# Two transformer blocks on one core: three gated tiles earlier, two memory-key tiles later, a spare expert half-slot free from the start

## What is computed

```
# first block
conv_out = conformer_conv(u_conv, ...)
attn_out = diff_attention(q, k, v, lam, ...)      # o = rms_norm(o, subln_g) per head
merged = gates[0] * (conv_out @ w_conv_out) + gates[1] * (attn_out @ w_attn_out)
x = x + merged @ w_out
h = rms_norm(x, ffn_norm_g)
x = x + hierarchical_moe(h, ...)                  # 32 experts: silu(x w_g[e]) * (x w_u[e]) @ w_d[e]
# second block
h = x
h = h + concat(mixers(rms_norm(h) @ w_in)) @ w_out
k, v = split(rms_norm(mem) @ w_kv, 2)             # memory keys and values, both 256 x 1024
h = h + softmax(q k^T) v @ w_o
h = h + conv_ffn(rms_norm(h))
return rms_norm(h)
```

## Time and profile before

| what | us |
|---|---|
| median of three runs | 1063.77 (1061.4 to 1064.07) |
| the profiled execution, by its own clock | 1061.16 |
| its span, first to last instruction | 1059.4 |
| PE busy in the span | 923.3 (87%) |
| DVE, ACT busy | 479.9 (45%), 356.7 (34%) |
| mean granted clock of TensorE | 0.939 |
| HBM read in the span | 298.9 MB |

### The profile page before, as it was taken

The page is one execution under the profiler, slowest core; times in us unless marked ns, Lnnn a source line. Parts: engine busy times, 40 slices in busy tenths (PEclk is TensorE's granted clock), DMA queues, the critical chain, the costliest instruction groups (busy, mean ns, idle before and its releaser), DMA issues.

```text
span 1059.4 us, 14271 instructions
## 1 busy us (share of the span) xinstructions
PE 923.3 (87%) x6038; PEld 669.1 (63%) x6038; DVE 479.9 (45%) x782; ACT 356.7 (34%) x569; POOL 1.3 (0%) x5
## 2 busy tenths in 40 slices
PE   7999998999889875867666776899999999999998
PEld 6969777964236431312222131389999989999986
DVE  6799867531001010010101010188866676888842
ACT  5442465131000010100000010258765745665632
POOL 0000000000000000000000000000000000000000
PEclk9999998999989997978887796999999999999999
DMA  9786230799999999999999999972334244565451
GB/s 319 272 297 244 101 119 13 296 395 421 426 411 425 419 427 424 426 427 424 427 423 429 424 428 423 406 273 81 111 128 160 80 160 160 161 207 189 160 198 40
DMA packets 76908, 300.80 MB, mean 284 GB/s; under 512 B 3761, under 2 KB 30514, under 8 KB 60210
## 3 DMA queue, kind: packets, MB, share of 16 engines
q1 hardware_dynamic: 75536, 298.89, 71.7%
q10 hardware_dynamic: 1314, 1.07, 0.4%
HBM read 298.90 MB, written 1.05 MB: 283 GB/s over the span
## 4 chain that ended last, share of the span: by engine, by line
PE 60%; DMA 27%; DVE 8%; ACT 2%; issue 1%; SPq 1%; DVEq 0%; PEldq 0%; ACTq 0%
PE bank L1361 11%; DMA ring<-in_w_down_e_dram 8%; DMA ring<-in_w_gate_e_dram 8%; DMA ring<-in_w_up_e_dram 8%; PE bank L1023 7%; PE bank L1379 6%; PE bank L1150 3%; PE bank L1243 3%; PE bank L1258 3%; PE bank L755 3%; PE bank L691 3%; PE bank L664 3%; PE bank L1076 3%; DMA qvpr<-in_w_down_e_dram 3%; DVE qvpr L1817 2%; DVE big L1916 2%
## 5 line engine op out<-in xcount | busy, mean ns | idle before, releaser
L1023 PE MATMUL bank<-ring,big 128*32 128x512 f32 x768 | 167.9, 717 | 80.9 <-DMA ring<-in_w_up_e_dram 43.0
L1023 PEld LDWEIGHTS bank<-ring,big 128*32 128x32 f32 x768 | 38.9, 127 | 202.4 <-issue 92.7
L346 DVE TENSOR_TENSOR ring_parts<-ring,ring_parts 128x2048 fp32r<-128x2048 f32 (+1 forms) x54 | 118.8, 2248 | 37.8 <-ACT ring_parts L338 37.5
L338 ACT ACTIVATE ring_parts<-ring 128x2048 fp32r<-128x2048 f32 (+1 forms) x54 | 98.5, 1874 | 53.9 <-DMA ring<-in_w_up_dram 26.0
L1361 PE MATMUL bank<-mrg_parts,ring_parts 128*128 128x256 f32 x640 | 82.3, 281 | 0.0
L2167 DVE TENSOR_TENSOR xT<-bank,xT 128x512 f32<-128x512 f32 x32 | 22.1, 692 | 130.6 <-PE bank L1062 130.6
L1361 PEld LDWEIGHTS bank<-mrg_parts,ring_parts 128*128 128x128 f32 x640 | 78.5, 189 | 0.0
L2121 DVE TENSOR_TENSOR big<-big,const 128x128 f32<-128x128 f32 x16 | 4.0, 289 | 154.4 <-PE bank L1010 154.3
L1023 PE MATMUL bank<-hs,big 128*32 128x512 f32 x128 | 70.9, 708 | 0.0
L1023 PE MATMUL bank<-qvpr,big 128*32 128x512 f32 x112 | 63.8, 725 | 1.1 <-DMA qvpr<-in_w_gate_e_dram 1.1
L2163 DVE TENSOR_TENSOR big<-bank,big 128x512 f32<-128x512 f32 x8 | 5.5, 692 | 120.2 <-PE bank L1023 120.2
(11 more groups left out here) (411 smaller groups left out, 1662.1 us busy)
## 6 DMA issues: line engine op xcount, KB each, us to landing
ring<-in_w_up_e_dram SPq DMA_DIRECT2D x24, 2048.0 KB, 29.0
ring<-in_w_gate_e_dram SPq DMA_DIRECT2D x24, 2048.0 KB, 22.0
ring<-in_w_down_e_dram SPq DMA_DIRECT2D x20, 2048.0 KB, 23.6
ring<-in_w_in_dram SPq DMA_DIRECT2D x12, 2048.0 KB, 15.0
ring<-in_w_up_dram SPq DMA_DIRECT2D x22, 1024.0 KB, 7.1
qvpr<-in_w_down_e_dram SPq DMA_DIRECT2D x5, 2048.0 KB, 20.4
ring<-in_w_down_dram SPq DMA_DIRECT2D x5, 2048.0 KB, 8.0
ring<-in_w_out_dram SPq DMA_DIRECT2D x4, 2048.0 KB, 8.4
```

Of the source, the lines that this page charges most:

```text
L338: signal(act.activation(pairs[stage][u % 3][0][:, part], raws[stage][u % 3][:, part], ACT.Copy), stage + "_hi")
L346: signal(eng.tensor_tensor(lo[:, part], raws[stage][u % 3][:, part], hi[:, part].bitcast(F32), ALU.subtract), name)
L1023: mm = pe.matmul(bank[part][CAP * j:CAP * j + CAP, :], xeT[:, c, CAP * j:CAP * j + CAP], w[j][c], start=(c == 0), stop=(c == DC - 1))
```

## The change

There are three edits.

1. `gated_conv(range(5, 8))` moves into the loop over the two head norms, behind the first.
2. Key tiles 4 and 5 leave the router's time and the tables' place. A half unit (1 MiB) is loaded at the end of turn 0 into the slot behind `KEY_UNIT`, and PE makes both tiles behind tiles 0 to 3. `RING_SHIFT` becomes 3, so that turn 1 starts one slot later. Where PE made tile 4 it now does 12 matmuls whose results nobody reads, and 4 of them where it made tile 5.
3. The tables' place is for the spare half unit alone: `load_spare(1)` stands first in `first_turn`, with no wait of its own. DVE waits for the counting matmuls before it frees `QVP`.

```diff
-            sp.dma_start(keys_w, w_xkv[:, :, 512:768]).then_inc(S["keys_early"], 16)
...
+                load_spare(1)
                 load_unit(0, 4)
...
                 load_unit(0, 7)
-                sp.wait_ge(S["keys_read"], 1)
-                load_spare(1)
                 load_unit(0, 8)
...
+                s, turn = LAST_KEYS
+                sp.wait_ge(used[s], turn + 1)
+                sp.dma_start(expert_slots[s][:, 0:2048].rearrange("p (k n) -> p k n", k=8), w_xkv[:, :, 512:768]).then_inc(landed[s], 16)
...
-        RING_SHIFT = 2
+        RING_SHIFT = 3
...
-            mem_keys((4,))
+            b = begin(pe, ("idle", 0))
+            for _ in range(12):
+                mm = pe.matmul(b[:, 0:T], ident, const[:, 0:T], start=True, stop=True)
+                tell(mm)
             pe.wait_ge(S["member"], 1)
...
-            mem_keys((5,))
+            for _ in range(4):
+                mm = pe.matmul(b[:, 0:T], ident, const[:, 0:T], start=True, stop=True)
...
                 pe.wait_ge(S["keys_full"], 4)
                 pe.sem_inc(used[s], 1)
-                pe.wait_ge(S["keys_out"], 4)
+                pe.wait_ge(S["keys_out"], 3)
+                s, turn = LAST_KEYS
+                pe.wait_ge(landed[s], 16 * (turn + (2 if s < PRELOADED else 1)))
+                w = expert_slots[s][:, 0:2048].rearrange("p (k n) -> p k n", k=8)
+                for i in range(2):
+                    for k in range(8):
+                        mm = pe.matmul(bank[0][:, T * i:T * i + T], w[:, k, P * i:P * i + P],
+                                       qko[:, k * T:k * T + T], start=(k == 0), stop=(k == 7))
+                mm.then_inc(S["keys_full"], 1)
+                pe.wait_ge(S["keys_full"], 5)
+                pe.sem_inc(used[s], 1)
+                pe.wait_ge(S["keys_out"], 5)
...
                 signal(dve.scalar_tensor_tensor(out=x, in0=x, scalar=st[:, 105:106], in1=r,
                                                 op0=ALU.mult, op1=ALU.mult), "attn_out")
-            gated_conv(range(5, 8))
+                if i == 0:
+                    gated_conv(range(5, 8))
...
+            arrive(dve, ("cnt", 0))
             dve.sem_inc(used[QVP], 1)
```

More of the change, by code:

```diff
@@ L107, in psum_plan @@
     uses += some("co", 4, 5) + some("on", 0, 2) + some("co", 5, 8) + some("mT", 0, 4) + some("ao", 0, 8) + [("rb", 0)] + some("wo", 0, 4) + some("rt", 0, 2) + some("wo", 4, 8)
-    uses += [("n2", 0)] + [None] * 3 + some("h2t", 0, 4) + some("kx", 4, 5)
-    uses += some("pos", 0, 2) + [("cnt", 0)] + some("kx", 5, 6)
+    uses += [("n2", 0)] + [None] * 3 + some("h2t", 0, 4) + [("idle", 0)]
+    uses += some("pos", 0, 2) + [("cnt", 0)]
     uses += [None] * (-len(uses) % 8)
@@ L936, in _ @@
                 scores(use, [(0, NE, C(a), mem[t], i == 0, i == len(terms) - 1) for i, (a, t) in enumerate(terms)])
-            mem_keys((5,))
+            for _ in range(4):
+                mm = pe.matmul(b[:, 0:T], ident, const[:, 0:T], start=True, stop=True)
+            filled(mm, ("idle", 0))
+            pe.sem_inc(empty[PLACE[("idle", 0)][0]], 1)
             GATHER_BANKS = (5, 6)
-            late = [("kx", 5), ("cnt", 0)]
+            late = [("cnt", 0)]
             assert not any(PLACE[use][0] in GATHER_BANKS for use in late)
-            for use in [("h2t", i) for i in range(4)] + [("mT", i) for i in range(4)] + [("rt", 0), ("rt", 1), ("n2", 0), ("kx", 4), ("pos", 0), ("pos", 1)]:
+            for use in [("h2t", i) for i in range(4)] + [("mT", i) for i in range(4)] + [("rt", 0), ("rt", 1), ("n2", 0), ("pos", 0), ("pos", 1)]:
                 copied(pe, use)
@@ L957, in _ @@
             pe.wait_ge(S["pick_step"], 2)
-            assert len(freed) == 1
+            assert not freed
             gather()
@@ L1556, in _ @@
             signal(act.activation(e_gap, e_gap, ACT.Exp), "e_exp")
-            for m in range(4, 6):
-                move(("kx", m), att[:, (8 + m) * T:(9 + m) * T], T)
             act.sem_inc(S["y_out"], 1)
@@ L1593, in _ @@
                                    ACT.Copy).then_inc(S["vx_out"], 1)
-            for j in range(2):
+            for j in range(3):
                 act.wait_ge(S["keys_full"], 3 + j)
-                act.activation(att[:, (8 + 2 * j) * T:(10 + 2 * j) * T], bank[j][:, :], ACT.Copy).then_inc(S["keys_out"], 1)
+                act.activation(att[:, (8 + 2 * j) * T:(10 + 2 * j) * T], bank[j % 2][:, :], ACT.Copy).then_inc(S["keys_out"], 1)
             act.wait_ge(S["rounds"], 1)
```

15 lines of the change are left out of this document (3 added, 12 removed).

## The result

The changed kernel takes 1068.39 us (median, 1065.62 to 1071.3) where the kernel before takes 1063.92 (1061.4 to 1065.38): ratio 1.0046, 95% interval 1.0033 to 1.0060, or 4.5 us slower. Its profiled execution spans 1067.1 us against 1059.4, 7.7 more.

What follows compares the result with a forecast made beforehand. DMA bytes at 422 GB/s bound the experts' stage; the order of PE and DVE sets the time elsewhere. Terms -2.8, +3.6 and +2.6 sum to +3.4 us, put on 1063.77: 1067.2 us, range 1061.5 to 1071.5.

Steps and rivals of the forecast that it cites:

- the 0.3% line: About 3.2 us, what a measurement tells from no change; chances given: slower 0.45, the same 0.48, faster 0.07.
- Part A: Head norms: gated tiles between the norms let PE begin L664's 32 records 5.0 us earlier, the clock staying up.
- The rival of two clock drops: Head norms: the pause there lowers the clock as well, PE ends L664 3 us later; +6.4, 1070.2 us; chance 0.12.
- Part B: Router: fewer key matmuls, so the gather begins 1.3 us earlier still and the first gate matmuls 6.1 us earlier.
- Part C: Start of the experts' stage: the unbroken run of transfers begins 6.7 us earlier (6.0 to 7.0); its bytes add 2.5.
- Part D: End of turn 0: PE is 7.0 us later for the late keys, so the DMA queue stands empty for 1.4 us.
- idle time above 2 us: Clock rule behind the second block's stall: pauses of 2.63 and 3.14 us lowered the clock, one of 1.95 did not.
- Part E: Second block's first load: it waits for the last down unit's slot, PE starts 11.55 us behind the landing: +3.6 us.
- Part F: Second block's start: PE stands still 3.5 us and the clock falls to 0.50: +2.6 us, bounds 0 and 3.4.
- the absorbed case: Second block: its later stages take up the stall and the clock's loss, 1061.0 us or 1059.6; chance 0.08.
- The clock did not hold, so that rival: Second block's start: the clock holds through the stall ahead of the first load; +0.8, 1064.6 us; chance 0.15.
- the one without a dry spell: End of turn 0: the DMA queue does not run empty; +2.0, 1065.8 us; chance 0.18.

Runs made afterwards that it cites:

- gates only: The kernel before with edit 1 alone (three gated tiles between the head norms): 1058.79 us, ratio 0.9959; again 1058.75 us, 0.9967.
- the kernel with two late matmuls: The changed kernel with only 2 of the 16 matmuls for key tiles 4 and 5, half unit still loaded: 1064.65 us, ratio 1.0011 to the kernel before.

## Why the prediction held, and where it did not

The median is 1.2 us above the forecast of 1067.2, inside the range. With 4.5 us the change is above the 0.3% line, where I had .45, and .48 below it. The mechanisms were right, but the sizes of three terms were off, and that the sum came so near is in part luck. By a sign that the prediction itself names, it failed in the middle: the experts' stage was not to end later than at 678.5, and the last down unit landed at 682.05, or 679.9 with 2.15 taken off.

- **Part A** held: 5.0 us (170.40 with gates only, where 170.5 stood), and the clock stayed up through the 1.21 us. The rival of two clock drops did not come.
- **Part B** held: gates 6.1 us earlier relative, 6.1 predicted.
- **Part C** held at its start: the run begins near 226.1 instead of 230.6, that is 6.6 us relative, with 6.7 predicted. But at the landing of turn 0's last down unit only 5.7 are left (309.74 against 313.28). Gates only shows the same loss: 5.1 at the gates, 4.1 at 309.14. I took the whole head start as carried through, which was about 1 us too much; no run here separates what took it.
- **Part D** was mis-sized, and this is the step that failed: 1.4 us predicted, bounds 0 and 2.5; 3.3 in the changed kernel's profile, 3.3 to 6.7 in seven executions, 3.7 by the medians of the kernel with two late matmuls. The margin of 3.1 us was about 1.5. I counted it to the landing that PE waited for at 363.05, but what runs dry is the stream of bytes, which thins out and ends earlier. The rows at 679:682 show such an end: 328, 188 and 25 GB/s, which at 422 GB/s would have been through by 680.3, while PE sees the landing at 682.05. That is about 1.8 us, an estimate for the place at 363. Then PE's new piece is 0.30 + 7.14 = 7.44 us with its wait, not 7.0. With 1.5 to spare, 7.4 - 2.5 - 1.5 = 3.4, and 3.3 were measured. The dip from 354 to 357 adds nothing to this: the down units flow when PE lets SP issue them, and a dip ahead of that only shortens the dry spell.
- The prediction put nothing in Part D for the clock. It took the stop of 1.95 us ahead of turn 1's gates as harmless, since the clock held there in the kernel before. Behind the same stop it fell in five of the other executions, and each fall on this stretch costs the late keys another 1.7 us. The "idle time above 2 us" that the prediction names as the point of decision does not hold either: the clock fell behind 1.95, and it held behind 2.47 at 123.03 in the kernel before itself.
- So the last down unit landed 0.1 us later relative, not 2.8 earlier. Parts C and D both made the change look better than it is.
- **Part E** held: 11.57 us behind the landing, 11.55 predicted. The experiment that moves the load brings it back to 7.94.
- **Part F** held as a mechanism (0.50 behind a stop of 3.47 us, gone when the stop is filled). Its size by the rows is 5.41 less 3.62, 1.8 us, in the changed kernel's first execution and 6.63 less 3.62, 3.0, in its second, on both sides of the 2.6 that I took. Parts E and F together are 5.4 and 6.7 in the two traces, and 5.2 by the medians. Filling the stop brought no time, so by the runs' times the clock's share of these can't be told from nothing.
- Nothing was taken up behind 770 us; the absorbed case is refuted. The clock did not hold, so that rival is out too, as is the one without a dry spell: in none of the executions with all 16 matmuls did the queue stay fed.
- The sum of the first trace is 0.1 + 5.4 = 5.5, that of the second, whose head norms stand where they stood before, 4.0 + 6.7 = 10.7; the medians say 4.5 and 6.9 (by the ratios 1.0046 and 1.0055, 4.9 and 5.8 us), where I had 3.4. Of the 5.2 us between the two traces 3.4 are the two falls of the clock in turn 0. The dry queue, 2 to 5 us larger than its term, is the main difference.

## What to carry to other kernels

When a ring of slots is shifted or lengthened by one, look at the load behind the loop: it goes to a slot by number, and if that slot is now the last one read, a whole transfer's latency stands on the path. Work put between two stages of a kernel that lives by its transfers is free only while bytes are still queued. Count its length against those bytes and not against the last landing, and where the margin is thin, count a fall of the clock as possible: here 1.5 us were to spare, and one fall cost 1.7. And time the halves of a combined change apart: here one alone was worth 4 us, and the other gave back twice that.

## What the runs showed of the hardware

**The same stop lowers the clock in one execution and not in the next.** In the first block PE waits for DVE, in all kernels with the same code and for the same time. Kernel before:

```profile
123.03 1.13 PE L812 MATMUL bank<-big,const 128*128 128x256 f32 x4 [2.47 <-DVE big L1916]
124.00 3.62 PE L664 MATMUL bank<-hs,ring 128*128 128x256 f32 x16
```

The changed kernel, and its clock in that stretch:

```profile
123.49 1.13 PE L814 MATMUL bank<-big,const 128*128 128x256 f32 x4 [2.46 <-DVE big L1922]
124.46 5.30 PE L666 MATMUL bank<-hs,ring 128*128 128x256 f32 x16
```
```profile
125.00:127.00 2.00, 2.00 (x6) 1.53 (x6) 1.89 (x5) 0.62 (x2) 0.00 (x0) 0.50 0.00 0
```

1.7 us more for one product, at 1.2 GHz. It happened in nine of the fourteen profiled executions, among them the changed kernel's first and the second of gates only, and not in those of the kernel before, of the first of gates only and of the changed kernel's second. The stop of 1.95 us ahead of turn 1's gates is of the same kind: the clock held behind it in the changed kernel's first execution and fell in the second. A stop of 2 to 2.5 us is thus a risk of some 1.7 us, not a fixed price, and a single profile can carry it in either direction: that is the 2.15 us (with 0.46 by which the first load landed later) between the two profiles compared here. It also is a likely reason, though not shown run by run, why the times of the changed kernel spread over 5.7 us.

**A queue that has run dry loses more than its standstill.** In [362:365] the changed kernel moved 63 GB/s, some 2.5 us of full rate, though nothing at all moved in only about 1.5 us of it.
